# Two token tiles of a product-key expert layer: gathered expert rows against a streamed full table

## What is computed

```
...
q = (xb @ w_q).reshape(tb, PEER_HEADS, 2, PEER_HALF)
s = jnp.einsum('thpc,pkc->thpk', q, sub_keys)
sv, si = lax.top_k(s, PEER_TOPK)
cand = sv[:, :, 0, :, None] + sv[:, :, 1, None, :]
cv, ci = lax.top_k(cand.reshape(tb, PEER_HEADS, PEER_TOPK * PEER_TOPK), PEER_TOPK)
i1 = jnp.take_along_axis(si[:, :, 0], ci // PEER_TOPK, axis=-1)
i2 = jnp.take_along_axis(si[:, :, 1], ci % PEER_TOPK, axis=-1)
experts = i1 * PEER_NKEYS + i2
gate = jax.nn.softmax(cv, axis=-1)
act = jax.nn.gelu(jnp.einsum('thkd,td->thk', u_tab[experts], xb), approximate=False)
w = gate * act
return jnp.einsum('thk,thkd->td', w, v_tab[experts])
...
```

## Time and profile before

| | us |
|---|---|
| median of 3 runs | 1933.88 |
| lowest, highest | 1932.89, 1934.9 |
| span of the profiled execution | 1935.4 |
| TensorE busy | 1671.8 |
| VectorE busy | 1388.6 |
| ScalarE busy | 536.9 |
| GpSimd busy | 667.4 |

### The profile page before, as it was taken

The page is one execution under the profiler, slowest core; times in us unless marked ns, Lnnn a source line. Parts: engine busy times, 40 slices in busy tenths (PEclk is TensorE's granted clock), DMA queues, the critical chain, the costliest instruction groups (busy, mean ns, idle before and its releaser), DMA issues.

```text
span 1935.4 us, 17829 instructions
## 1 busy us (share of the span) xinstructions
PE 1671.8 (86%) x5443; PEld 999.0 (52%) x5443; DVE 1388.6 (72%) x3413; ACT 536.9 (28%) x1215; POOL 667.4 (34%) x605
## 2 busy tenths in 40 slices
PE   8999999999879899898888989877777878788777
PEld 7888987887545555554544555423322212333233
DVE  5998684228887777777788777777777777777754
ACT  3121142113333343333223233322222122222222
POOL 0020030004334433433345444444444444434442
PEclk9989999999989999999998999998999888989999
DMA  5452475558998999999999999999999999999996
GB/s 210 142 88 98 152 148 157 182 185 356 404 395 360 418 419 418 418 416 415 419 385 419 421 420 403 421 419 410 415 418 421 407 421 407 417 418 416 419 413 281
DMA packets 112687, 675.14 MB, mean 349 GB/s; under 512 B 12784, under 2 KB 15296, under 8 KB 42576
## 3 DMA queue, kind: packets, MB, share of 16 engines
q0 software_dynamic: 80816, 577.23, 73.6%
q1 hardware_dynamic: 31216, 95.87, 14.3%
q10 hardware_dynamic: 560, 0.92, 0.2%
HBM read 665.79 MB, written 6.21 MB: 347 GB/s over the span
## 4 chain that ended last, share of the span: by engine, by line
PE 43%; DMA 36%; DVE 8%; issue 8%; POOL 2%; ACT 2%; ACTq 0%; POOLq 0%; DVEq 0%
DMA upper<-in_peer_uv,upper 18%; DMA lower<-in_peer_uv,upper 17%; PE pair L1187 17%; PE pair L681 7%; PE pair L692 6%; PE pair L1044 4%; DVE upper L2119 3%; PE pair L795 2%; DVE lower L2119 1%; POOL upper L657 1%; ACT upper L1589 1%; POOL lower L657 1%; PE pair L990 1%; PE pair L726 1%; PE pair L807 1%
## 5 line engine op out<-in xcount | busy, mean ns | idle before, releaser
L1187 PE MATMUL pair<-upper 128*128 128x512 f32 (+1 forms) x1144 | 572.4, 643 | 139.8 <-ACT upper L1589 139.7
L657 POOL DMA_INDIRECT upper<-in_peer_uv,upper x324 | 380.0, 1173 | 503.5 <-PE pair L1187 440.4
L1187 PE MATMUL pair<-lower,upper 128*128 128x512 f32 (+1 forms) x772 | 376.3, 627 | 88.6 <-ACT upper L1589 88.6
L1187 PEld LDWEIGHTS pair<-upper 128*128 128x128 f32 (+1 forms) x1144 | 219.0, 198 | 421.7 <-issue 275.7
L657 POOL DMA_INDIRECT lower<-in_peer_uv,upper x220 | 248.0, 1127 | 473.7 <-PE pair L1187 292.0
L2119 DVE CUSTOM_DVE_ANT_0 upper<-upper 128x1024 f32<-128x1024 f32 x172 | 210.7, 1225 | 120.8 <-DMA upper<-in_peer_uv,upper 120.8
L1187 PEld LDWEIGHTS pair<-lower,upper 128*128 128x128 f32 (+1 forms) x772 | 144.5, 194 | 272.1 <-issue 182.7
L1589 ACT ACTIVATE upper<-upper 128x128 f32<-128x128 f32 (+1 forms) x479 | 160.7, 386 | 292.7 <-DVE upper L2135 292.5
L2119 DVE CUSTOM_DVE_ANT_0 upper<-upper,lower 128x1024 f32<-128x1024 f32 x152 | 185.6, 1222 | 71.1 <-DMA upper<-in_peer_uv,upper 70.4
L1397 ACT ACTIVATE upper<-upper 128x4 f32<-128x4 f32 (+1 forms) x141 | 41.8, 297 | 620.2 <-DVE upper L2119 620.0
L2119 DVE CUSTOM_DVE_ANT_0 lower<-lower,upper 128x1024 f32<-128x1024 f32 x116 | 142.2, 1226 | 85.7 <-DMA lower<-in_peer_uv,upper 85.7
(11 more groups left out here) (423 smaller groups left out, 1772.2 us busy)
## 6 DMA issues: line engine op xcount, KB each, us to landing
lower<-in_w_in SPq DMA_DIRECT2D x64, 512.0 KB, 7.3
lower<-in_peer_q SPq DMA_DIRECT2D x28, 512.0 KB, 8.0
lower<-in_proj SPq DMA_DIRECT2D x48, 256.0 KB, 7.2
lower<-in_w_out SPq DMA_DIRECT2D x16, 512.0 KB, 6.2
upper<-in_peer_uv,upper POOLq DMA_INDIRECT x324, 11.9
upper<-in_cache_k SPq DMA_DIRECT2D x8, 512.0 KB, 4.4
upper<-in_cache_v SPq DMA_DIRECT2D x8, 512.0 KB, 3.6
lower<-in_peer_uv,upper POOLq DMA_INDIRECT x220, 11.9
```

The lines of the kernel that those rows point to most:

```text
L657: pool.indirect_dma_start(row(g), None, a["peer_uv"], bass.IndirectOffsetOnAxis(ap=idx[:, n % 8, j:j + 1], axis=0)).then_inc(row_in[g % RI ...
L1187: mm = pe.matmul(pairs[n % 2][0:rows, h, :], diag[:, (nth - 1) % DIAGS, 0:rows], row(g)[:, D + h * 512:D + (h + 1) * 512], start=(j == min ...
```

## The change

Only tiles 0, 1 and 4 keep gathered rows: 18 jobs, 288 rows. VectorE adds no rows any more. Tiles 2 and 3 are handled at the end, densely:

1. Their 16 routes (`SPREAD`) run behind the dots of jobs 10 to 17, two more in each job; they leave indices i1, i2 and gate for 128 (head, choice) pairs of each token.
2. These are transposed, so that a column belongs to a token. For each of 256 tokens GpSimd makes a one-hot matrix of i1 (`first_hot`), VectorE a one-hot matrix of i2 times the gate (`second_hot`), and TensorE multiplies the two into a 128 x 128 share matrix of the token. Four tokens make a quad; 64 quads. ScalarE copies each out of PSUM into `dense_g`, with the token innermost.
3. All of U streams through as 128 blocks of 512 KiB: eight matmuls of 256 columns each give the product of 128 experts with 256 tokens. ScalarE takes the Gelu of a pair of blocks, VectorE multiplies by the shares. All of V streams through as 128 blocks: four matmuls of 512 columns each (two tiles, two halves). V comes two pairs behind U.
4. The normalised tokens `xn` need the inverse root of each token's mean square along the free axis, a new bank job `rq`. Tiles 2 and 3 no longer need `xt2` and `xt3`.

The second trunk's slots come faster: 7, 3, 3, 3 in four rows. It ends at row 183 instead of 268.

```diff
-EXPERTS = ([(t, h) for t in range(3) for h in range(PH)] + [(4, 0), (4, 1)] + [(3, h) for h in range(PH)])
+EXPERTS = [(t, h) for t in range(2) for h in range(PH)] + [(4, 0), (4, 1)]
 NJ = len(EXPERTS)
...
+SPREAD = [(t, h) for h in range(PH) for t in (2, 3)]
+ROUTES = {0: EXPERTS[1:3]}
+for _n in range(1, NJ):
+    ROUTES[_n] = EXPERTS[_n + LAG:_n + LAG + 1]
+    if _n >= NJ - PH:
+        _h = _n - (NJ - PH)
+        ROUTES[_n] = ROUTES[_n] + SPREAD[2 * _h:2 * _h + 2]
+STEPS = 32
...
 def late_matmuls(j):
-    return 5 if j % 4 == 3 else 2
+    return 7 if j % 4 == 3 else 3
...
+NI = 128
+QUADS = 64
+US, VS = 5, 4
+BEHIND = 2
+STREAM = []
+for _p in range(NI // 2 + BEHIND):
+    if _p < NI // 2:
+        STREAM += [("u", _p)]
+    if _p >= BEHIND:
+        STREAM += [("v", _p - BEHIND)]
...
             for n in range(NJ):
-                ways = first_routes() if n == 0 else route(n + LAG) if n + LAG < NJ else iter(())
+                ways = routes(n)
+                pace = -(-STEPS * len(ROUTES[n]) // (TOPK if n else 12))
...
+            for q in range(QUADS):
+                if q >= 2:
+                    pool.wait_ge(hot_done, q - 1)
+                for k in range(4):
+                    ins = pool.tensor_scalar(first_hot[:, q % 2, k, :], iota128, spread_i[:, 0, 4 * q + k:4 * q + k + 1],
+                                             None, ALU.is_equal)
+                ins.then_inc(first_ok, 1)
...
+            for q in range(QUADS):
+                pe.wait_ge(first_ok, q + 1)
+                pe.wait_ge(second_ok, q + 1)
+                if q >= 4:
+                    pe.wait_ge(dense_out, q - 3)
+                for k in range(4):
+                    mm = pe.matmul(quad(q)[:, P * k:P * k + P], first_hot[:, q % 2, k, :], second_hot[:, q % 2, k, :],
+                                   start=True, stop=True)
+                mm.then_inc(hot_done, 1)
...
+            pe.wait_ge(dense_out, QUADS)
+            for kind, p in STREAM:
+                if kind == "u":
+                    if p >= 4:
+                        pe.wait_ge(act_ok, p - 3)
+                    for i in (2 * p, 2 * p + 1):
+                        pe.wait_ge(*unit_in(i))
...
+                        for k in range(KD):
+                            mm = pe.matmul(quad(p)[:, FIRST * (i % 2):FIRST * (i % 2) + FIRST], unit_w(i)[:, k, :], xn[:, k, :],
+                                           start=(k == 0), stop=(k == KD - 1))
+                        mm.then_inc(unit_done, 1)
+                    continue
+                pe.wait_ge(dense_ok, p + 1)
...
+                for i, t in order:
+                    v = 2 * p + i
+                    pe.wait_ge(*value_in(v))
+                    for h in range(2):
+                        mm = pe.matmul(pairs[t][:, h, :], dense_pair(p)[:, i, P * t:P * t + P],
+                                       value_w[:, v % VS, 512 * h:512 * h + 512], start=False, stop=last and i == 1)
...
+            for q in range(QUADS):
+                act.wait_ge(hot_done, q + 1)
+                ps = quad(q).rearrange("p (t i) -> p i t", t=4)
+                for part in range(2):
+                    ins = act.activation(dense_g[part][:, :, 4 * q:4 * q + 4], ps[:, 64 * part:64 * part + 64, :], ACT.Copy)
+                ins.then_inc(dense_out, 1)
...
+            for q in range(QUADS):
+                if q >= 2:
+                    dve.wait_ge(hot_done, q - 1)
+                for k in range(4):
+                    n = 4 * q + k
+                    ins = ts(second_hot[:, q % 2, k, :], iota128, spread_i[:, 1, n:n + 1], spread_g[:, n:n + 1],
+                             ALU.is_equal, ALU.mult)
+                ins.then_inc(second_ok, 1)
```

More of the change, by code:

```diff
@@ L1173, in _ @@
                 rows = P if EXPERTS[n][0] < TILES else 32
-                mine = [j for j in range(TOPK) if j not in vector_rows(n)]
                 if n >= 2:
-                    pe.wait_ge(acc_step, ADDED[n - 2])
+                    pe.wait_ge(acc_step, n - 1)
                 for j in range(TOPK):
[L1178 to L1190, removed]
+                    g = TOPK * n + j
@@ L1191, in _ @@
+                    pe.wait_ge(diag_ok, g + 1)
+                    for h in range(2):
+                        mm = pe.matmul(pairs[n % 2][0:rows, h, :], diag[:, g % DIAGS, 0:rows],
+                                       row(g)[:, D + h * 512:D + (h + 1) * 512],
+                                       start=(j == 0), stop=(j == TOPK - 1))
+                    mm.then_inc(v_used, 1)
                     for _ in range(late_matmuls(j)):
                         next(late, None)
+            for _ in late:
+                pass
@@ L2231, in _, with routes @@
                 emptied(dve, f"xt{t}")
-            def first_routes():
-                for n in range(1, LAG + 1):
-                    yield from route(n)
+            def routes(n):
+                for t, h in ROUTES[n]:
+                    yield from route(t, h)
             def mean_of(t):
@@ L2295, in _ @@
                     pass
-            last = TOPK * NJ - 1
-            dve.wait_ge(v_used[0], V_USERS[last - 1][1])
-            dve.wait_ge(w_ok, len(GROUPS))
-            for half in range(2):
-                cols = slice(512 * half, 512 * half + 512)
-                stt(h2(3)[:, cols], row(last)[:, D + 512 * half:D + 512 * half + 512], weight[:, (NJ - 1) % 8, 15:16],
-                    pairs[(NJ - 1) % 2][:, half, :], ALU.mult, ALU.add).then_inc(acc_ok, 1)
-            dve.wait_ge(fsq_ok, finished + 2)
@@ L2304, in _ @@
-            ts(frs, fss, fss_b, D * RMS_EPS, ALU.add, ALU.add).then_inc(fms_ok, 1)
-            dve.wait_ge(frt_ok, finished + 1)
-            link(dve.reciprocal(frs, frs))
-            for half in range(2):
-                cols = slice(512 * half, 512 * half + 512)
-                stt(ytile[:, cols], h2(3)[:, cols], frs, gf[:, cols], ALU.mult, ALU.mult).then_inc(yt_ok, 1)
+            weigh(4 * NJ - 1)
+            dve.wait_ge(cexp, NJ + 1)
+            each = shares.rearrange("p t (h k) -> p (t h) k", k=TOPK)
```

371 lines of the change are left out of this document (232 added, 139 removed).

## The result

The changed kernel takes 2425.67 us (median), the kernel before 1933.51 beside it: ratio 1.254, 95% interval 1.252 to 1.256. Three of its four runs took 2424.24 to 2425.75 us at a mean granted clock of 0.955 to 0.958, and the fourth, of which there is no profile and which the ratio leaves out, took 3026.13 us at 0.738. The forecast was 2414, in a range of 2310 to 2510.

A forecast was written before the change was run, and what follows sets the result against it. Gathers bound the kernel before; in the changed one TensorE, then VectorE, were to bind, and TensorE the stream. Last dot 1390 + turnaround 15 + one-hots 115 + 4 + stream 882 + tail 10 = 2416 us profiled, 2414 median; range 2310 to 2510.

The forecast's parts named there:

- Stream, 882 us: Streaming U and V at the end: U's matmuls 442 us, V's 440, all on TensorE, with transfers hidden.
- rivals 3 (lower clock): In the stream: 1.2 GHz doubles a matmul, each tenth of the stream costs 88 us; from 2500 us up; chance 0.06.
- 4 (closer matmuls): In the stream: matmuls closer than the series showed, bound by weight loads of 0.19 us; 2118 us in all; chance 0.03.
- Trunk, 617 us of matmuls: Gathers under the second trunk, up to row 183: TensorE's V products and late trunk take 617 us, transfers 542.
- 37 us of waits: Up to row 183: TensorE waits for diagonals, taken as 0.2 us a row, between 0 and 88 us in all.
- Three routes, 47 us a job: Gathers after the second trunk: VectorE sets the pace, a job with three routes taking 47 us against 40 of transfers.
- A row of gathers, 2.48 us: Expert stage of the kernel before: 2.48 us per 1 MiB row, so the 256 removed gathers gain 635 us.
- One-hot matrices, 115 us: The 64 quads between gathers and stream: 1.8 us each, 115 us in all, bounds 78 to 151.
- rival 2: VectorE and GpSimd exclude each other in the one-hot products: 36 us more, 2450 us in all; chance 0.15.
- GpSimd's 1.14 us a quad: One-hot products: GpSimd's four operations per quad, priced from a nearest row of 285 ns for 128 columns.
- Rival 1: Gathers keep the transfers' pace, TensorE and VectorE fitting beside them: last dot at 1252 us, end at 2276; chance 0.13.
- Rival 5, the other side: Stream at its transfers' pace, 321 us: 1855 us in all, 4% faster; turning point 6.3 us a pair; chance 0.02.

The follow-up runs named there:

- experiment 5: The changed kernel with the stream's operands (U, V, tokens, weighted shares) rounded to bfloat16, sums and loads still float32: 1868.75 us, ratio 0.965 to the kernel before.
- Experiment 3: The changed kernel with tile 3's routes left out and tile 2's choices copied in their place: 2410.26 us (one run).
- six and two: The changed kernel with VectorE making six and GpSimd two one-hot matrices per quad instead of four and four: 2371.45 us, ratio 1.226 to the kernel before.

## Why the prediction was right, and where it was not

**Stream, 882 us: right.** The prices of a matmul, 0.432 and 0.86 us, gave 13.8 us a pair, and 13.77 were measured, with clock 1.00 and no gaps; experiment 5 shows that these matmuls are the cause. The pace from starts in the earlier trace rows carried it; by the records' means, which overlap, U alone would come out longer. For the profiled execution rivals 3 (lower clock) and 4 (closer matmuls) fall by the same row. The sustained 131 ns for 512 columns of the Trainium skill (TensorE: Matmul & The Clock Gate, "Back-to-back issue gap") was not seen: the starts of records of 512 columns stand 0.43 us apart in the stream, and 0.215 in bfloat16 in experiment 5.

**Trunk, 617 us of matmuls: right; 37 us of waits: wrong.** From 462.25 us the matmuls alone lead to 1079, and the last late score ended at 1083. TensorE was busy 595.98 of 600 us. The step that failed is the 0.2 us a row for diagonals, a choice between two bounds: beside a trunk that fills TensorE it should have been near 0. That the waits before were waits for late gathers fits this, since the transfers no longer bind here, but no run shows it by itself.

**Three routes, 47 us a job: right.** From 1115 to 1265 us the trace has 102 records of the dots in 150 us. Each dot is two records, so 2.94 us a row and 47 us a job; job by job it is 46.8, 46.7, 46.6 and 47.9. From the end of the trunk to the last dot the forecast has 274 us, and 280 were measured, so the trunk's 33 us less these 6 are the 27 by which the last dot is early. Experiment 3 adds what the prediction did not say, that another bound is close behind: of the seven us that part 47 from the transfers' 40 about three were won.

**A row of gathers, 2.48 us: misread.** The 242 gathers are the sum of twelve answers the earlier trace rows, and one that lies across a border is in two of them. A single answer over 1300 to 1900 us has 237, so 2.53 us a row: the removed gathers are worth 648 us instead of 635. VectorE's price of a row rests on the same count, and the forecast would move by some 5 us, so this decides nothing.

**One-hot matrices, 115 us: wrong.** 154 us, beyond the upper bound of 151, and by another mechanism than rival 2. The step that failed is GpSimd's 1.14 us a quad, taken from an affine select of 285 ns. Its compare with a column as scalar measured 0.585 us, so 2.34 a quad. The prediction said that no row had this operation; the average between two bounds was then a choice without a reason, and a bound from another operation was no bound. VectorE was priced too high: 0.305 an operation, 0.25 measured when it was full.

**Rival 1 (gathers keep the transfers' pace, 2276)** falls: the DMA share was 0.96 beside the trunk and 0.92 behind it, and the last dot came at 1362.8, not at 1252. **Rival 5, the other side**, fell for the changed kernel and came true in experiment 5. Its turning point of 6.3 us a pair fits: at 5.13 us the kernel is 65 us faster than before, which puts the point at 5.13 + 65 / 64 = 6.1.

## What to carry to other kernels

Before a gather is replaced by a dense stream, work out the matmuls of one block in the type that they will have, from the distance of starts in a steady series, and set them against the block's transfer: here 13.8 us of matmuls against 5.1 of transfers lost, and 3.5 against 5.1 won. A small operation that runs hundreds of times on an engine where it has never run is measured first, by itself. When a bound is removed, look how near the next one stands: a route less moved the last dot by 12.5 us where 25 to 33 were expected, and the transfers had been at 0.92 already.

## What was not expected of the hardware

The granted clock fell to 0.71 in the one-hot stretch, where TensorE was busy 72 us in each 100 in short pieces, and it cost nothing. The timeline of TensorE in the changed kernel, one line for each quad's share matrices (eight records):

```profile
1400.28 2.07 PE L1265 MATMUL pair<-upper 128*128 128x128 f32 x8 [0.23 <-POOL upper L709]
1402.68 1.95 PE L1265 MATMUL pair<-upper 128*128 128x128 f32 x8 [0.33 <-POOL upper L709]
1404.99 1.16 PE L1265 MATMUL pair<-upper 128*128 128x128 f32 x8 [0.35 <-POOL upper L709]
1407.31 1.16 PE L1265 MATMUL pair<-upper 128*128 128x128 f32 x8 [1.16 <-POOL upper L709]
```

The same eight records take 2.07 us and, two quads later, 1.16. The granted clock is 0.51, the lower level of 1.2 GHz, from 1400.0 to 1404.5 us, and 1.00, the upper of 2.4 GHz, from 1404.9 to 1409.5; yet the quads come 2.3 to 2.4 us apart throughout, at GpSimd's pace. With six and two, TensorE was busy about as much of the time (37.28 of 50 us), at clock 1.00.

VectorE's product of 512 columns took 0.69 us in the stream, where the prediction had 1.07 from the earlier trace rows. The 1.07 belongs to L1817 of the kernel before, a step of the scan that reads every eighth element, as L1822 does; L1821 between them, the same shape read in order, takes 0.69 there too:

```profile
L1822 DVE TENSOR_TENSOR upper<-upper 128x512 f32<-128x512 f32 x7 | 7.6, 1086 | 0.2
...
L1821 DVE TENSOR_TENSOR upper<-upper 128x512 f32<-128x512 f32 x7 | 4.8, 692 | 0.2
```

That the step between elements is the cause is not shown, since no run changes it alone. It hides either way.
